# A two-block model in one kernel: where the modulation weights are read, and the embedding normalised by chunks

## The reference

```
h = _layer_norm(concat([meta, x]), emb_ln_g, emb_ln_b)      # the embedding
for li in range(2):                                         # the two layers of the first block
    proj = h @ w_in[li] ; mixed = ... ; h = _layer_norm(ALPHA * h + mixed, ...)
    ff = _hier_moe(h)                                       # top 2 of 32 experts per token
    h = _layer_norm(ALPHA * h + ff, ln2_g, ln2_b)
# second block: silu(c), silu(c_ctx) times w_mod [1024, 6 * 1024], plus b_mod:
# six groups of 1024 numbers for the tokens, and for the context rows.
#   groups 0, 1: shift and scale of the mixer's norm    group 2: gate of the mixer
#   groups 3, 4: shift and scale of the feed-forward's norm    group 5: gate of the feed-forward
```

## Time and profile before

| | |
|---|---|
| three runs | 3643.62, 3648.4, 3661.0 us; median 3648.4 |
| profiled execution | 3663.72 us, its span 3661.9 us |
| TensorE busy | 3146.8 us, 86% |
| VectorE, ScalarE, GpSimd busy | 1715.8, 894.9, 525.4 us |
| moved by DMA | 421.60 MB, mean 115 GB/s |
| mean granted clock of TensorE | 0.923 of full |
| prelude | from the start to about 87 us |
| `combine`, first and second layer | 1106 to 1150 us, 2182 to 2224 us |
| `scale_inputs` | 2225.8 to 2255.3 us |

### The profile page before, as it was taken

One profiled execution on the slowest core, in us unless ns is written; L12 is line 12 of the kernel. 1 busy time (PEld: TensorE's weight loads), 2 busy tenths in 40 slices (PEclk: granted clock), 3 DMA queues, 4 the chain that ended last, 5 costly groups with the idle time before them and its releaser, 6 DMA issues. The chain is left out here.

```text
span 3661.9 us, 69839 instructions
## 1 busy us (share of the span) xinstructions
PE 3146.8 (86%) x29370; PEld 2305.4 (63%) x29370; DVE 1715.8 (47%) x3124; ACT 894.9 (24%) x1896; POOL 525.4 (14%) x806
## 2 busy tenths in 40 slices
PE   5899799977874899799958756999989899999998
PEld 1666599754443666698745433566656688778843
DVE  3344566541113445466441115455567776576601
ACT  3111333221113112233121114133354210122200
POOL 0000355001101000454001120000045300000000
PEclk7999699988996999799979987999999999999999
DMA  8210300229995110300249992110010122222221
GB/s 320 77 35 19 156 13 5 83 102 365 394 383 125 35 35 27 140 4 5 82 189 369 405 321 69 59 35 24 18 54 1 58 81 92 82 69 86 73 71 47
DMA packets 175422, 421.60 MB, mean 115 GB/s; under 512 B 25796, under 2 KB 122436, under 8 KB 146580
## 3 DMA queue, kind: packets, MB, share of 16 engines
q1 hardware_dynamic: 156147, 383.22, 28.4%
q0 software_dynamic: 8736, 17.32, 2.0%
q10 hardware_dynamic: 10240, 16.79, 1.4%
HBM read 400.55 MB, written 50.54 MB: 123 GB/s over the span
## 5 line engine op out<-in xcount | busy, mean ns | idle before, releaser
L2085 PE MATMUL ps<-e_w,e_xt 128*64 128x256 f32 x1792 | 230.6, 415 | 63.1 <-DMA e_w<-in_moe_w 61.6
L2085 PEld LDWEIGHTS ps<-e_w,e_xt 128*64 128x64 f32 x1792 | 151.6, 150 | 163.1 <-issue 77.4
L745 PE MATMUL ps<-h,win 128*128 128x264 f32 x960 | 233.6, 397 | 16.5 <-DVE pad L894 14.9
L2192 DVE TENSOR_TENSOR e_hid<-ps,e_silu 64x256 f32<-64x256 f32 x64 | 39.4, 615 | 395.5 <-ACT e_silu L2151 395.5
L745 PEld LDWEIGHTS ps<-h,win 128*128 128x128 f32 x960 | 181.0, 193 | 67.2 <-issue 38.3
L3582 PE MATMUL ps<-ff_up,wt 128*128 128x512 f32 x352 | 152.2, 592 | 0.0
L3522 PE MATMUL ps<-h_lat,wt 128*128 128x256 f32 x544 | 133.4, 388 | 14.5 <-DMA wt<-in_w_in 7.7
L1473 DVE COPY_PREDICATED inv<-level,ps 112x384 f32<-112x384 int32 x176 | 103.7, 589 | 78.9 <-PE ps L1385 70.6
L3522 PE MATMUL ps<-h_lat,w_sums 128*128 128x256 f32 x544 | 130.1, 382 | 0.0
L2104 PE MATMUL ps<-e_w,e_hid_t 128*64 128x512 f32 x448 | 111.0, 614 | 20.3 <-DMA e_w<-in_moe_w 13.4
L1385 PE MATMUL ps<-inv,nt 48*48 48x48 f32 x3520 | 124.0, 209 | 5.1 <-issue 3.9
(11 more groups left out here) (615 smaller groups left out, 6616.4 us busy)
## 6 DMA issues: line engine op xcount, KB each, us to landing
e_w<-in_moe_w SPq DMA_DIRECT2D x168, 1024.0 KB
wmod<-in_w_mod SPq DMA_DIRECT2D x24, 1024.0 KB, 13.5
early<-in_moe_w SPq DMA_DIRECT2D x24, 1024.0 KB, 12.0
wt<-in_w_up SPq DMA_DIRECT2D x22, 1024.0 KB, 5.1
y_rows<-e_y ACTq DMA_DIRECT2D x128, 128.0 KB
win<-in_w_in SPq DMA_DIRECT2D x10, 1536.0 KB, 6.7
wt<-in_w_in SPq DMA_DIRECT2D x12, 1024.0 KB, 5.2
wt<-in_w_down SPq DMA_DIRECT2D x16, 704.0 KB, 4.8
```

The source lines that it names most:

```text
L745: last = pe.matmul(ps[:, 7, 0:HT], lhsT=ring[(s + 1) % 2][:, i, o:o + P], rhs=k.h[:, i, h * HT:(h + 1) * HT], start=(i == 0), stop=(i == K ...
L2085: last = pe.matmul(ps[half, 2 + z, 0:EH], lhsT=xt[z][:, f, :], rhs=w[:, f, :], start=(f == 0), stop=(f == KD - 1))
L2192: dve.tensor_tensor(hid[z][high, :].rearrange("s (t q) -> s q t", t=2), ps[high, 2 + z, 0:EH].rearrange("s (q t) -> s q t", t=2), si[z][hi ...
```

## The change

The six groups are split over four places: groups 0, 1 and 5 in the prelude (3 x 8 pieces of 512 KB), group 2 in the first layer's `combine`, group 3 in the second layer's, group 4 in `scale_inputs`. A group's product is 4 matmuls of 256 columns per piece. The silu vectors `c_silu` now stay in SBUF.

```
+MOD_PARTS = 4
+SOON_MODS, LATE_MOD = (0, 1, 5), 4
+def mod_products(k, pe, tile, i, bank):
+    for q in range(4):
+        last = pe.matmul(k.ps[32 * q:32 * q + 2, bank, 0:256], lhsT=k.c_silu[:, i, :],
+                         rhs=tile[:, q * 256:(q + 1) * 256], start=(i == 0), stop=(i == KD - 1))
+    return last
...
 def prelude(k, a):
-        flat = sb("m_rows", [P, STRIPS, 512])
-        ring = [sb(f"wmod{i}", [P, WIDE]) for i in range(RING)]
+        flat = sb("m_rows", [P, len(SOON_MODS), 256])
+        strip = [[sb(f"wmod{n}_{i}", [P, D]) for i in range(KD)] for n in range(len(SOON_MODS))]
...
+                for n, g in enumerate(SOON_MODS):
+                    for i in range(KD):
+                        sp.dma_start(strip[n][i][:, :], w[:, i, g * D:(g + 1) * D]).then_inc(wmod_in[n * KD + i], 16)
                 sp.wait_ge(blanked, 4)
...
-                for n in range(RING, N):
-                    stream(n)
-                    for dst, src in grid[2 * (n - RING):2 * (n - RING) + 2]:
-                        sp.dma_start(dst, src).then_inc(grid_in, 16)
+                for dst, src in grid:
+                    sp.dma_start(dst, src).then_inc(grid_in, 16)
                 sp.wait_ge(grid_in, 16 * 24)
...
+                pe.wait_ge(consts_in, 16 * 6)
+                for x in range(len(SOON_MODS) * KD):
+                    n, i = x // KD, x % KD
+                    if x >= 4 and x % 2 == 0 and (x - 4) // 2 < NC1:
+                        turn_rows((x - 4) // 2)
+                    pe.wait_ge(wmod_in[x], 16)
+                    last = mod_products(k, pe, strip[n][i], i, BANK + n)
```

```
+                def norm(j):
+                    dve.wait_ge(emb_root, j + 1)
+                    dve.reciprocal(st[:, 3, j:j + 1], st[:, 3, j:j + 1]).then_inc(emb_inverted, 1)
+                    dve.wait_ge(emb_inverted, j + 1)
+                    dve.tensor_scalar(rows[:, j, :], rows[:, j, :], st[:, 1, j:j + 1], st[:, 3, j:j + 1],
+                                      ALU.add, ALU.mult).then_inc(emb_ready, 1)
...
+def mod_place(k, i):
+    return k.early[1 + i // 6][i // 2 % 3][:, :, :].rearrange("p a b -> p (a b)")[:, i % 2 * D:(i % 2 + 1) * D]
+def load_mod(k, a, li, sp, i):
+    sp.dma_start(mod_place(k, i), mod_weights(a)[:, i, bass.ds((li + 2) * D, D)]).then_inc(k.mod_in[i // 2], 16)
...
 def combine(k, a, li, cb, gate, dest):
+        @block.sync
+        def _(sp):
+            sp.wait_ge(landed[3], 32)
+            for i in range(KD):
+                load_mod(k, a, li, sp, i)
...
             for j in range(NC1):
+                if j == 3:
+                    products(0, KD // 2)
+                elif j == 4:
+                    products(KD // 2, KD).then_inc(streamed, 1)
                 pe.wait_ge(normed, j + 1)
-                if j >= 4:
-                    pe.wait_ge(act_kept, j - 3)
-                    pe.wait_ge(dve_kept, j - 3)
+                if j >= 2:
+                    pe.wait_ge(act_kept, j - 1)
+                    pe.wait_ge(dve_kept, j - 1)
...
+                if j == 4:
+                    pe.wait_ge(strip_kept, 1)
+                    turn_mods(k, pe, flat, 4).then_inc(strip_turned, 1)
...
                 if j:
                     finish(j - 1)
+                if j == 4:
+                    act.wait_ge(streamed, 1)
+                    act.activation(flat[0:98, 0, :], ps[0:98, BANK, 0:256], ACT.Copy).then_inc(strip_kept, 1)
+                    act.activation(k.mod[:, 2 * KD:3 * KD, :], k.mod[:, 3 * KD:4 * KD, :], ACT.Copy).then_inc(shifted, 1)
+            act.wait_ge(strip_turned, 1)
+            act.wait_ge(shifted, 1)
+            for v in range(2):
+                act.activation(mods_at(k, 3, v), turned_mods(k, v, 4), ACT.Copy)
             finish(NC1 - 1)
...
 def scale_inputs(...):
+            for i in range(KD):
+                sp.dma_start(strip[i][:, :], mod_weights(a)[:, i, LATE_MOD * D:(LATE_MOD + 1) * D]
+                             ).then_inc(late_in[i], 16)
...
+            dve.wait_ge(streamed, 1)
+            dve.tensor_copy(flat[0:98, 0, :], ps[0:98, 6, 0:256]).then_inc(strip_kept, 1)
+            for g in (2, 3):
+                for v in range(2):
+                    dve.tensor_tensor(mods_at(k, g, v), mods_at(k, g, v), mod_bias(k, g), ALU.add)
+            dve.wait_ge(strip_turned, 1)
+            for v in range(2):
+                chain(dve.tensor_tensor(mods_at(k, LATE_MOD, v), turned_mods(k, v, 1), mod_bias(k, LATE_MOD), ALU.add))
+            make_gain(k, dve, 2, 4, 0, "norm_ffn")
```

More of the change, by code:

```diff
@@ L352, in sb, with place @@
             return k.sb(name, shape, dt, stack=tmp)
+        def place(j, f):
+            b, n = (0, f) if f < ACT_TILES else (1, f - ACT_TILES)
+            return k.h[:, f, j * TC:(j + 1) * TC], ps[:, 2 * (j % 2) + b, n * TC:(n + 1) * TC]
         rows = sb("rows", [TC, NC1, D])
@@ L467, in _ @@
+                pe.wait_ge(strip_kept, len(SOON_MODS))
+                for n in range(len(SOON_MODS)):
+                    last = turn_mods(k, pe, flat, BANK, n)
+                last.then_inc(strip_turned, 1)
             @block.scalar
@@ L1739, in moe @@
         with ExitStack() as cb:
-            combine(k, cb, gate, dest)
+            combine(k, a, li, cb, gate, dest)
         k.right.close()
@@ L2211, in _, with combine @@
             keep(*in_loop(n_turns, -1), True)
-def combine(k, cb, gate, dest):
+def combine(k, a, li, cb, gate, dest):
     nc, ps = k.nc, k.ps
@@ L2406, in _ @@
             last.then_inc(summed_ctx, 1)
+            for i in range(KD):
+                pe.wait_ge(late_in[i], 16)
+                last = mod_products(k, pe, strip[i], i, 6)
+            last.then_inc(streamed, 1)
+            pe.wait_ge(ctx_kept, CT)
+            pe.wait_ge(strip_kept, 1)
+            turn_mods(k, pe, flat, 1).then_inc(strip_turned, 1)
         @block.gpsimd
```

220 lines of the change are left out of this document (106 added, 114 removed).

## The result

The changed kernel takes 3632.1 us, the median of 5 runs (3628.0 to 3636.2). The kernel before, run beside it on the same chip, takes 3652.4 (3643.6 to 3661.8). The ratio is 0.9935, with a 95% interval from 0.991 to 0.9961: 24 us faster, between 14 and 33. The same pair measured again, with more runs, gave 3632.3 against 3660.7, ratio 0.9925 [0.9906, 0.9943]. The forecast was 26.2 us less, and it lies in both intervals.

A forecast was written before the change was run, and what follows sets the result against it. The prelude was taken as bound by its weight transfers, TensorE bounding most of the rest. Prelude -30.0, combining +3.2 and scaling +0.6 gave -26.2 us, from the median 3648.4 to 3622, range 3610 to 3639.

The forecast's parts named there:

- First piece and spacing: Prelude: first 512 KB weight piece at 20.5 us, the others 1.22 us apart, the last at 49.6.
- rival B: Pieces with 4 KB rows run as slowly as the embedding rows: 13 us slower, or 3649 if only the prelude; chance 0.05.
- The weights' chain: Prelude: last weight piece, its matmuls, then copy, turns and additions, ending at 53.2 us.
- SyncE's grids: Prelude: 24 small transfers now queued behind all weights; their landing at 56.0 us ends the prelude's work.
- rival E: Weights' chain, not the grids, ends the prelude, 2.8 us more saved; clock stays up in scaling; about -33, 3615; chance 0.10.
- The saving of the prelude: Half the weights go from the prelude: layer's first load at 58.2 us for 88.19, 30.0 saved.
- Embedding by chunks: Prelude: one pass per chunk, VectorE through by 42 us, sines by 43, hidden behind the weights; no cost, no gain.
- Combining stage: ScalarE waits for the products: 1.5 us per layer plus 0.1 for semaphores, 3.2 us for both layers.
- Rival A: Combining stage: pieces and gather hamper each other, 5 to 8 us lost per layer, 3629 to 3635; chance 0.13.
- Rival D: Combining stage: ScalarE behind late products; at 17 us per layer the kernel is 4.6 slower, 3653; chance 0.03.
- Scaling stage: Eight 512 KB pieces behind the projection weights, products in TensorE's idle gap: cost 0.6 us, from 2 gained to 6 lost.
- Rival C: Fixed cost per queued transfer, 2.43 to 3.2 us per prelude piece: 3652 to 3664; chance 0.03.

The follow-up runs named there:

- the second profile: The changed kernel profiled once more, no edit, beside the kernel before: 3632.3 us, ratio 0.9925.
- the loads-only kernel: Changed kernel whose combining stages issue their eight loads but multiply, copy and turn nothing, with no scaling-stage part: 3629.6 us, one run.
- the kernel with three edits: Changed kernel with grid loads moved to the layers' first stage, token rows as 80 + 8, ScalarE's product copy behind chunk 5's square and root: 3620.0 us.

## Why the prediction was right, step by step

**First piece and spacing.** Forecast 20.5 and 1.22; measured 19.85 (18.66 in the second profile) and 1.22. The 1.9 us for constants and positions ahead of the weights were too much by 0.65 or more. The price put aside for rows of 4 KB, 1 us, can't be told from the grids: the last piece came at 50.64 for 49.6, and in the kernel with the grids gone at 49.12. Rows of 4 KB are as fast as rows of 8 KB (1.22 us for half of what took 2.43, and 412 GB/s over 24 us), as the earlier trace rows said and rival B did not.

**The weights' chain** was to end at 53.2 and ended at 53.86. **SyncE's grids** were to end the prelude at 56.0 and did at about 56.4. The issue times were less good: the last weight piece was issued at about 34.3 (forecast 36), and the queue then held single issues for 3.6 us. The order of the two chains, which was the choice that the number rested on, is shown by the move of the grids: 4.6 us, where the 2.8 named with rival E leave out the traffic. Rival E's condition is not met in the changed kernel.

**The saving of the prelude**: forecast 30.0, measured 29.2, and 30.2 by the second profiles. The exit was taken as 2.2 and is 2.6.

**Embedding by chunks**: forecast nothing, VectorE through at 42 and the sines at 43. VectorE's last copies start at 42.68 and end at 44.43, the sines end at 43.8. So it is up to 2.4 us later than forecast, and the sign "through before 43" is not met, but 9 us of cover are left and the cost is nothing, as forecast. The old order gives the same first load.

**Combining stage**: forecast 1.5 us per layer by ScalarE standing in line behind the products, and 0.1 for the exit. The mechanism is there: with ScalarE out of the line, all but 0.1 us of the cost is gone. The size was too large: 0.96 and 0.07 in one execution, -0.13 and 0.61 in the next; over the twelve layers with this order it is -0.36 to 1.61, 0.33 in the mean. Two assumptions failed. One is that all eight products run at the lower clock. The other is that all of ScalarE's delay reaches the end: VectorE waits only 0.8 of ScalarE's 1.3 us in the first layer, since in the kernel before it was still at its own copies when ScalarE's root was done. And in three of the twelve layers the last turn ran at the higher clock, which gave 0.6 back; the forecast has the clock only as the lower end of this term. Turn 3 was to be hidden behind the pieces or nearly; it was 0.48 late. The pieces landed a little later than forecast, the last 9.0 us behind chunk 2's turn for 8.4. The half rate that the gather was to have beside them cost nothing, if it had it: with the loads alone the stage takes 15.59 and 15.57. What was left out is the exit of the first layer, 1 us and not 0.05. Together some 2 us against 3.2.
Rival A (5 us and more per layer) is out by the loads-only kernel: no delay at all from the transfers, though they share the engines with the gather. Rival D is ScalarE's place in the line as well, but with products that end 24 us behind chunk 2's turn; they ended 10.6 and 8.3 us behind it.

**Scaling stage**: forecast +0.6; measured 29.5 and 29.6 against 29.8 and 28.9, no cost or gain within 0.9. A closer measure is from ScalarE's root for the tokens (`n_st`) to the next stage's first matmul: 17.36 to 17.37 in the five profiles without this part, 17.56 to 17.57 in seven of the eight with it (17.65 in the other). The cost is 0.2 us. Behind its context scaling VectorE works 1.4 us longer, for 1.6 forecast, and the next stage begins 0.3 us behind its end, for 0.5. The gain of the clock, which was named as the other side of the range, is not shown: the next stage's first matmuls still run at the lower clock.

**Rival C** (a fixed cost per transfer) is out by the spacing of 1.22 us and by the 1 MiB pieces. The Trainium skill, "DMA: Bandwidth & Descriptors", section "Bandwidth", asks for transfers of 1 MiB or more. The formula that the prediction takes with it stands in the same page's section "Anatomy of one DMA — SWDGE (gpsimd) path", as a fit for single transfers issued by GpSimd; applied to SyncE's queue, as the prediction did, it makes the prelude with half the transfer size 12 us longer than the old one, an estimate, and it was 29 shorter.

**Rival E's sum.** Its -33 doesn't come out of its own terms: 32.8 saved, 3.2 and 0.6 paid and up to 2 from the clock make -31. The lower end of the range rests on it.

**The sum.** Forecast -26.2; by the stages -29.2 + 2 + 0.2 is -27, the profiled spans differ by 27.5, and the two ratios give -24 and -27.5. That it comes so near is in part luck: the prelude is within 1 us of its term, the two costs were each put too high, the exit too low, and the layers, which have no term, moved by up to 7 us either way. That the plain medians give -20 and -28 is the scatter of single executions (before: 3643.6 to 3669.4). The absolute time, 3632 for 3622, is off by 10 us. In the first round 4 of these are the median of before, 3652.4 for the 3648.4 on which the forecast stood, and 6 the smaller difference of the medians; in the last round before has 3660.7, which is 12 more, with a difference larger by 2.

## What to carry to other kernels

A stretch that waits for transfers at the queue's best rate (393 to 418 GB/s here) is priced by bytes: bytes that are moved to a stage with room for them are a gain of bytes over that rate, and here the receiving stages paid under a tenth of it. The DMA share alone doesn't tell: the gather had 0.99 at 168 GB/s, and 4.2 MB more went beside and behind it at no cost. After such a change, look for what the queue carries behind the large transfers: small loads whose issues were hidden between big ones became the end of the stage, and moving them gave another 4.6 us. Put a wait for the moved work behind, not ahead of, the instruction on which the next engine waits (0.4 us per layer in the mean here, up to 1.5). Read such an effect from the stage, in several profiles, since one execution of the stage moved by up to 2 us and executions of the whole kernel by some 25.

## What the hardware showed that was not expected

Token rows of 88 partitions slow down the queue behind them. From 12 to 16 us the rate was 208 to 246 GB/s with the DMA share full; with the same rows as 80 + 8 it rose two us earlier, from 211 to 366 GB/s at 14 us, and the first weight piece was used at 17.30 for 19.85 (16.82 in the kernel with three edits, 18.55 at the earliest with 88 rows). The Trainium skill, "DMA: Bandwidth & Descriptors", section "Why a DMA increments its semaphore by 16 and not by 1", says that a transfer is spread over the largest number of engines up to 16 that divides its outermost size: 11 for 88 rows, 16 for 80. The direction agrees. The size doesn't follow from it alone, since 11 of 16 engines at the later 392 to 412 GB/s would be some 270 to 280 GB/s, an estimate, and from 12 to 14 us the 80 + 8 kernel is no faster (227 and 211 GB/s for 246): what is gained is an earlier end of the slow stretch, and why it is slow at all stays open.

The queue's hold on SyncE comes in lumps: one small table held it for 3.60 us (35.48) and the second group of eight small triangles took 3.71, 0.46 each, when the queue had room. The transfers of the moved pieces and a gather by GpSimd's queue went together without a delay to the gather: 414 GB/s in 1106 to 1108, when only pieces were left, and 207 GB/s while the gather ran (windows of the changed kernel's combining stage):

```profile
1098.00:1100.00 2.00, 0.00 (x0) 0.00 (x0) 1.93 (x5) 2.00 (x6) 0.00 (x0) 0.50 1.03 207
...
1106.00:1108.00 2.00, 1.99 (x20) 1.17 (x22) 1.97 (x5) 2.00 (x5) 0.00 (x0) 0.50 1.03 414
```
